# Moving the large SBUF tiles to multiples of 512 bytes, and other warm-up matmuls ahead of two norms

## The reference

```python
h = LN1(alpha*h + 0.5 * swiglu(h, w1_gate, w1_up, w1_down))     # hidden width 5632
h = LN2(alpha*h + mixer(h))                                     # projections, attention, merge, w_o
h = LN3(alpha*h + 0.5 * swiglu(h, w2_gate, w2_up, w2_down))
```

## Time and profile before

| | |
|---|---|
| median of 3 runs | 2341.22 us (2339.74 to 2344.0) |
| span of the profiled execution | 2340.8 us |
| TensorE busy | 2271.0 us, 97% |
| VectorE, ScalarE, GpSimd busy | 54%, 41%, 8% |
| mean granted TensorE clock | 0.985 |
| DMA | 419.72 MB, 179 GB/s |

### The profile page before, as it was taken

The page is one execution under the profiler, slowest core; times in us unless marked ns, Lnnn a source line. Parts: engine busy times, 40 slices in busy tenths (PEclk is TensorE's granted clock), DMA queues, the critical chain, the costliest instruction groups (busy, mean ns, idle before and its releaser), DMA issues.

```text
span 2340.8 us, 27742 instructions
## 1 busy us (share of the span) xinstructions
PE 2271.0 (97%) x10293; PEld 1856.9 (79%) x10293; DVE 1274.9 (54%) x1153; ACT 955.7 (41%) x1095; POOL 177.0 (8%) x67
## 2 busy tenths in 40 slices
PE   9999999999999698999999999997999999999997
PEld 7888888878887587888888888866888888878885
DVE  5555545544444747575675456556555455544445
ACT  4344344433333444443344444352444444433333
POOL 1000000000000523030150000004000000000001
PEclk9999999999999799999999999998999999999998
DMA  7656656655555356655455566644566565566553
GB/s 254 198 179 198 189 186 190 187 170 189 188 180 185 92 170 198 192 148 170 144 164 152 171 195 203 197 142 132 183 192 190 182 195 181 183 216 188 187 188 126
DMA packets 221174, 419.72 MB, mean 179 GB/s; under 512 B 14896, under 2 KB 23856, under 8 KB 220336
## 3 DMA queue, kind: packets, MB, share of 16 engines
q1 hardware_dynamic: 221104, 418.78, 57.4%
HBM read 416.63 MB, written 2.10 MB: 179 GB/s over the span
## 4 chain that ended last, share of the span: by engine, by line
PE 94%; DVE 4%; ACT 1%; issue 1%; DMA 0%; ACTq 0%; SPq 0%; DVEq 0%
PE acc L420 30%; PE acc L422 30%; PE acc L421 29%; DVE w_lo L406 2%; PE bank L455 1%; PE bank L1491 1%; DVE act_lo L866 1%; PE bank L1444 1%; PE bank L1344 0%; PE bank L1465 0%; ACT w_hi L401 0%; PE acc L1541 0%; PE acc L1542 0%; PE acc L1543 0%; PE bank L1448 0%
## 5 line engine op out<-in xcount | busy, mean ns | idle before, releaser
L406 DVE TENSOR_TENSOR w_lo<-raw,w_hi 128x1024 fp32r<-128x1024 f32 x776 | 995.4, 1301 | 623.9 <-ACT w_hi L401 617.0
L401 ACT ACTIVATE w_hi<-raw 128x1024 fp32r<-128x1024 f32 x776 | 810.1, 1058 | 911.8 <-PE acc L422 869.6
L420 PE MATMUL acc<-w_hi,act_hi 128*128 128x512 f32 x2240 | 896.1, 400 | 39.6 <-DVE act_lo L866 35.2
L422 PE MATMUL acc<-w_hi,act_lo 128*128 128x512 f32 x2240 | 879.8, 393 | 0.0
L421 PE MATMUL acc<-w_lo,act_hi 128*128 128x512 f32 x2240 | 878.0, 392 | 0.0
L420 PEld LDWEIGHTS acc<-w_hi,act_hi 128*128 128x128 f32 x2240 | 424.1, 189 | 129.1 <-DVE act_lo L866 38.5
L422 PEld LDWEIGHTS acc<-w_hi,act_lo 128*128 128x128 f32 x2240 | 423.9, 189 | 92.3
L421 PEld LDWEIGHTS acc<-w_lo,act_hi 128*128 128x128 f32 x2240 | 424.6, 190 | 84.9
L422 PE MATMUL acc<-w_hi,hT_lo 128*128 128x512 f32 x704 | 280.9, 399 | 0.0
L421 PE MATMUL acc<-w_lo,hT_hi 128*128 128x512 f32 x704 | 277.4, 394 | 0.0
L420 PE MATMUL acc<-w_hi,hT_hi 128*128 128x512 f32 x704 | 276.2, 392 | 0.9 <-DVE hT_lo L855 0.9
(11 more groups left out here) (191 smaller groups left out, 998.9 us busy)
## 6 DMA issues: line engine op xcount, KB each, us to landing
raw<-in_ffn_w_gate_dram SPq DMA_DIRECT2D x176, 512.0 KB, 4.5
raw<-in_ffn_w_up_dram SPq DMA_DIRECT2D x176, 512.0 KB, 4.4
raw<-in_ffn_w_down_dram SPq DMA_DIRECT2D x176, 512.0 KB, 4.0
raw<-in_w_in_dram SPq DMA_DIRECT2D x176, 512.0 KB, 3.8
raw<-in_w_o_dram SPq DMA_DIRECT2D x32, 512.0 KB, 5.1
raw<-in_w_branch_a_dram SPq DMA_DIRECT2D x16, 512.0 KB, 4.9
raw<-in_cmp_k_w_dram SPq DMA_DIRECT2D x8, 512.0 KB, 4.1
raw<-in_cmp_v_w_dram SPq DMA_DIRECT2D x8, 512.0 KB, 4.8
```

The source lines that it names most:

```text
L401: nc.scalar.activation(w_hi[:, r, :], raw[:, r, :], ACT.Copy).then_inc(hi_done, 1)
L406: nc.vector.tensor_tensor(w_lo[:, r, :], raw[:, r, :], w_hi[:, r, :].bitcast(F32), ALU.subtract).then_inc(lo_done, 1)
L420: nc.tensor.matmul(o, ah, hi, start=first and k == 0, stop=False)
L422: mm = nc.tensor.matmul(o, al, hi, start=False, stop=last and k == SLOT_KT - 1)
```

## The change

Two edits. The small tables are declared ahead of `raw`, and a pad is put behind them:

```diff
-WARM_START, WARM_H, WARM_LN = 2, 4, 6
+WARM_START, WARM_H = 2, 4
+WARM_MIX = ((0, 0, P), (0, 16, P), (0, 32, P), (16, 0, P))
+WARM_F = ((8, 0, P), (0, 8, P), (0, 0, 66), (32, 64, P))
...
+        small = sb("small", [P, TILES * N_CMP + TILES + P])
+        vec_rows = sb("vec_rows", [64, P])
+        pos_rows = sb("pos_rows", [CMP_BLOCK, 2, P])
+        vecT = sb("vecT", [P, 4 * KT + 2 * CMP_BLOCK])
+        stats = sb("stats", [P, TILES, OUT_CHUNKS, 6])
+        ln_s = sb("ln_s", [P, 8, TILES])
+        mv = sb("mv", [P, TILES, 2])
+
+        at = 1152 + 4 * (160 + 128 + 256 + 128 + 48 + 16 + 8)
+        if at % 512:
+            sb("pad", [P, (512 - at % 512) // 4])
         raw = sb("raw", [P, RING, SLOT])
...
         affine = sb("affine", [P, 2, 2, TOKENS])
-        small = sb("small", [P, TILES * N_CMP + TILES + P])
...
-        mv = sb("mv", [P, TILES, 2])
```

And the six float32 matmuls at the two inner norms become twenty fp32r matmuls in four groups of five. Each group has its own offsets, in elements of 4 bytes, of the loaded operand (a) and the streamed one (b), and n columns loaded:

```diff
+            def warm_rounded(offsets):
+
+                for a, b, n in offsets:
+                    for _ in range(5):
+                        nc.tensor.matmul(bank[0:n, 3, :], act_lo.rearrange("p k n -> p (k n)")[:, a:a + n],
+                                         act_hi.rearrange("p k n -> p (k n)")[:, b:b + COLS], start=True, stop=True)
...
                 if f:
                     wait_bank_free(pe, T[("x", f, 3)])
-                    keep_warm(WARM_LN, 3)
+                    warm_rounded(WARM_F)
...
                             wait_bank_free(pe, T[("x", "mix", 3)])
-                            keep_warm(WARM_LN, 3)
+                            warm_rounded(WARM_MIX)
```

## The result

| | before | after |
|---|---|---|
| median | 2342.61 us of 4 (2339.74 to 2344.19) | 2320.15 us of 4 (2318.12 to 2323.05) |
| profiled span | 2340.8 us | 2316.3 us |

The ratio is 0.9907, 95% interval 0.9895 to 0.9919: 22 us or 0.93% off, where I had forecast 2324.4 and 0.7%. A second measurement of the same kernel later gave 2322.07 us and 0.9918 (0.9905 to 0.9932). The profiled spans differ by more, 24.5 us. Each timed execution on record took about 1.8 us more than its span, so the profiled execution of the kernel before took some 2342.6 us by estimate, slower than the 2341.22 us median of the first three, and the profiled one after was the fastest of its four (2318.12 us).

What follows compares the result with a forecast made beforehand. The prediction took TensorE's matmul spacing as the bound (busy 97% of 2340.8 us). 14.08 + 1.92 + 0.84 = 16.8 us off gave a span of 2324.0 and a median of 2324.4 us, 0.7% faster, range 2317 to 2333.

Steps and rivals of the forecast that it cites:

- Bound and path: Whole kernel: TensorE's matmul spacing sets the time; VectorE and the loads do not bite at 2.72 us a slot.
- Down projections: Two down projections: 176 slots go from 2.80 to 2.72 us with `hT` loaded, 14.08 us off.
- Branches: Branches with `oT` loaded: 96 groups go from 700 to 680 ns, 1.92 us off.
- hT at remainder 32: Down projections: the loaded operand's start, 32 bytes past a multiple of 512, makes groups take 700 instead of 680 ns.
- common starts collide: Rival, 4%: loaded and streamed operands both at remainder 0 slow every group; 2385 us.
- Streaming from `chunks` and `kT`: Float32 matmuls streaming these tiles: about 3 ns off each of 120 + 48 + 56 + 56 records, 0.84 us.
- The 2240 groups with `act` loaded: Groups moving from remainder 128 to 0: taken as no change, bounds +20 and -40 ns a group.
- Warm-ups at nothing: Both inner norms: twenty fp32r matmuls end 0.6 to 0.8 us earlier, idle grows to about 1.5 and 1.1, time unchanged.
- Clock +-3.4 us: Norms: one half-clock stretch more or fewer at each, such as that at 768.67 us; taken as 0.
- no effect of place: Rival, 8%: the 20 ns a group belong to something other than tile place; 2340 to 2341 us.
- remainder 128 as a loss: Rival, 5%: at remainder 0 the 40 ns a group over the column rate go too; 2203 us.
- Half an effect: Rival, 3%: aligned `hT` starts each slot at the wider spacing and recovers, 7 us given back; 2332 us.

Runs made afterwards that it cites:

- place_only: The changed kernel with the old six float32 warm-up matmuls put back at both norms, so only the new tile places remain; 2323.15 us, ratio 0.9923.
- all_32: place_only without the pad, so every large tile, streamed and loaded, starts 32 bytes past a multiple of 512; 2322.72 us, ratio 0.9919.
- ht_64: place_only with 64 bytes more ahead of `hT`, shifting it and all behind it against the streamed weights; 2338.09 us, ratio 0.9986.
- act_off: place_only with 32 bytes between `w_lo` and `act_hi`, so everything loaded starts at 32 and streamed weights at 0; 2375.32 us, ratio 1.0147.
- warm_only: The changed kernel with the small tables moved back behind `affine`, so old places with the new fp32r warm-ups; 2340.48 us, ratio 0.9998.
- no_warm: place_only without any warm-up matmuls ahead of the two inner norms; 2323.92 us, ratio 0.9928.
- one_pad: The kernel before with only 96 bytes of pad ahead of `hT`, putting all large tiles at remainder 128; 2324.62 us, ratio 0.9925.
- probe: The full change with 24 warm-up matmuls in each of 16 groups at varied offsets and columns; spacing 226.7 ns with both operands at 0, 233.3 at 32 bytes.

## Why the prediction was right, and where its reason was not

- Bound and path: right. Taking 80 ns from each of 200 slots makes 16.0 us, and place_only moved the end by 17.7; VectorE and the loads did not step in at 2.72 us a slot.
- Down projections, 14.08 us: 14.00 in the profile. Branches, 1.92: 1.67.
- The reason given for them, hT at remainder 32: only half of it. The argument that I used against the rival "common starts collide", that `w_hi` and `act_hi` have equal remainders and are the fast case, was the rule itself. all_32 shows that 32 is as good as 0 for all, ht_64 that 64 is as bad as 32 for one of two. That the forecast came out was luck in this respect: the change made everything equal. The same reasoning, an operand judged by its own start, would have failed on all_32 by the sign (2385 us against 2322.72, faster than before) and, where it takes 64 for as good as 128, on ht_64 by 15 us (2338.09 against place_only's 2323.15). On act_off it would have come out right, for the same half of a reason.
- Streaming from `chunks` and `kT`, 0.84 us: did not come. Both rows stay at a median of 275 ns though their tiles moved to 0 (against the earlier trace rows), so the 3 ns were not place; what they are was not tested. I had also read durations here, which are modelled: by their starts the back-to-back matmuls that stream `chunks_lo` were 111.4 ns apart before and 111.2 after, 0.04 us over all 280 records at that rate (an estimate).

```profile
L1504 PE MATMUL bank<-chunks_lo,pT x120: 270/275/275, 983.5 to 1235.7; 128*128 128x128 f32 x120
...
L1461 PE MATMUL bank<-kT,qT x56: 270/275/275, 933.9 to 1268.5; 128*128 128x128 f32 x56
```

- The 2240 groups with `act` loaded, at 0: right for the settled spacing, 680 ns. Not in my sum: groups near transposes. The some 1900 not interrupted average 682.2 ns before and 681.5 after, some 1.3 us. The stretch from the last matmul of the compression weights to the branches (444.91 us before) is 1.3 us shorter in after and in place_only alike. So the sum came near place_only's 17.7 us partly by luck: 0.84 us that did not come stood in for about as much that was not in it.
- Warm-ups at nothing: no run contradicts it; warm_only (0.9989 to 1.0007) and no_warm agree with it, and an effect of one or two us would not show. The cover held, with idle of 1.33 and 0.89 us for my 1.5 and 1.1.
- Clock +-3.4 us: too narrow for the profiled pair, which differs by 6.1 us in the stretches with waits. 2.3 of these are at the start of the span, where I had allowed for nothing; 2.4 are behind the first norm, where the stretch that I had named, at 768.67 us, went. Between medians it is less. place_only's 17.7 us (2340.89 - 2323.15) is the figure to hold against my 16.8; the first measurement of the full change had 4.7 us more than that (22.5), the second 1.5 more (19.3).
- Rivals: no effect of place, and remainder 128 as a loss, are out (one_pad has all at 128 and the full gain, and with all at 0 the settled group still takes 680 ns, not 640). "Half an effect" is out: of the 702 `hT` groups in the trace that another group follows at once, 695 take 680 ns. "Common starts collide" is the reverse of what happens.
- The Trainium skill (TensorE: Matmul & The Clock Gate, "Step-by-step: what each phase is for") says that, with two independent SBUF read ports, a load takes no read bandwidth from the running matmul. For fp32r with a load for each matmul this does not settle the spacing: in act_off 3040 groups lose 17 ns each on average by 32 bytes between the two operands. What in the hardware makes the two starts matter, no run shows.

## What to carry to other kernels

Where fp32r matmuls run back to back with a load each, lay the loaded and the streamed tiles at equal remainders of 256 bytes; it is worth 3% of such a stretch (226.7 against 233 ns) and costs a pad. Neither has to be at a multiple of anything: all at 0, at 32 and at 128 gave 2323.15, 2322.72 and 2324.62 us. Compare the spacing of stages that differ in one operand, and before naming a cause, list every property of the place that differs, the relation to the other operand included. Two stages of unequal pace fit several rules; shift one tile only, and shift all tiles together, and they part.

## What was not expected of the hardware

- The settled spacing is reached over several matmuls: up to nine wide spacings of 224 to 236 ns, then 227, 227, 226 repeating. Unequal pairs repeat patterns of their own (229, 238 at 384 bytes; 226, 229, 232 at 64) and stay there.
- The offset of 64 bytes costs least of the unequal ones in the probe (229.2 ns), but in ht_64, with three matmuls in turn on different tiles, the `hT` groups average 700.0 ns, as with 32 (act_off) and -96 (the kernel before).
- Loading fewer columns widens the spacing at equal starts: 230.0 ns at 96 and 64 columns, 231.7 at 32. Why, and what the 13.3 ns over the column rate are, stays open.
- Without the warm-ups the granted clock fell to 0.50 for 6.8 us at each inner norm, and the next stage's first matmul came no later (no_warm): the transposes' 1.4 us more went into a wait that was there anyway.
